# High weights by both activation halves as one product of 512 columns, in the feed-forward of a two-block transformer kernel

## The chip, the cores and the metric

One Trainium2 chip, one core. The metric is the device time of one execution in microseconds (us). The kernel before takes 2200.33 us (median of 3 runs, 2199.25 to 2201.02).

## What is computed

Two blocks over 256 tokens of width 1024 (and 256 context tokens in the first): a first block with attention, convolution and a mixture of 32 experts in each of two layers, then a second block of two hybrid layers. The edit is in the feed-forward of a hybrid layer:

```python
D_FF = 4 * D_MODEL            # 4096
def hybrid_layer(x, ..., w_ff1, w_ff2):
    ...
    hf = rms_norm(x, norm_g[2])
    ff = jnp.square(jax.nn.relu(hf @ w_ff1)) @ w_ff2
    return x + rms_norm(ff, norm_g[3])
```

All of it is in float32, and the kernel keeps that accuracy with products of rounded parts: a value x is split into high = rounded x and low = x - high, and a product w.x is the sum of w_high.x_high, w_high.x_low and w_low.x_high.

## The kernel before

The hybrid layers' weights are streamed in slabs of 128 x 4096 float32 (2 MB), one DMA each, into three ring places; a slab in use goes through `split_both` (L2987) on VectorE: a cast into `w_hi` (L2995; two places, used in turn) and a subtraction into `w_lo`, over the raw slab (L2996). The split of slab n+2 waits until TensorE is done with slab n.

The order of the feed-forward's slabs is written out in `FF_ORDER` (L87): first-half slabs (w = 1, eight a layer, 512 hidden units each) and second-half slabs (w = 2) alternate, as (1,0), (1,1), (2,0), (1,2), (2,1), ... (1,7), (2,6), (2,7). Slab (1,0) is done in `first_hidden` with tokens as output rows, and stays as it is.

For j = 1 to 7, `hidden(n, j)` (L2326) computes four chunks of 128 hidden units by 256 tokens, into the lower half (256 columns) of PSUM banks 4 to 7. A chunk is eight steps k, and a step is `three` (L1427): three products of 256 columns, L1429 (high weights by high activations), L1430 (high by low), L1431 (low by high). The activations are `hn_hi` (in the ring's last place) and `hn_lo` (in `hT`). TensorE signals each chunk by `f1_mm`.

VectorE's loop (L3182) takes the chunks of a first-half slab in order: L3192 takes the chunk m out of PSUM, max with 0 and times the row factor `rB`, into `sqb`, and signals `f1_ev`; ScalarE (L1386 to L1389) waits for that, squares in place and signals `ffh_ready`; VectorE then, after L3192 of chunk m+1, makes the parts of chunk m with `parts` (L3035): a cast into `ff_hi` (L3037), `link` (a wait for the instruction's own end), a subtraction into `ff_lo` (L3038). After a slab's four chunks VectorE goes on to the next `split_both`.

`output(n, j, b, h)` (L2346) multiplies `ff_hi` and `ff_lo` (as stationary operands) with a second-half slab, 48 products of 512 columns a slab, L2079 to L2081, into banks 0 to 3. At the end of a layer the order is: three quarters of slab (2,6), half of (2,7), the last quarter of (2,6), the rest of (2,7). `take` (L2083) makes TensorE wait until a slab is split.

In the same trace `h_lo` of the first mixer is `[P, TG, KC, NX]`, read as two runs of 256 columns with other data between, while `h_hi` is read as one run of 512.

Of the kernel before, what the change touches and what calls it, by code (L numbers as in the profile page):

```python
# [12 lines left out]
F32 = mybir.dt.float32  # L13
# [4 lines left out]
ALU = mybir.AluOpType  # L18
ACT = mybir.ActivationFunctionType
AX_X = mybir.AxisListType.X  # L20

P = 128
D = 1024
KC = D // P
NX = 256
# [60 lines left out]
SLAB = 4096  # L86
# [16 lines left out]
def hybrid_program(nc, xT_in, params_in, consts_in, invcnt_in, lparams_in, pos_in, w_static, ex_gate, ex_up, ex_down, w_layer, gains_in,  # L103
# [3 lines left out]
    lo, n_lp = offsets(LPARAMS)  # L107
    ctx = ExitStack()
    with ctx:
        address = {}  # L110
# [5 lines left out]
        def rounded(name, shape, over, column):  # L116

            return nc.alloc_sbuf_tensor_at(name, shape, FR, offset=address[over] + 4 * column)

        def sem(name):  # L120
            return ctx.enter_context(nc.semaphore(name))


        ring = sb("ring", [P, RING, SLAB])
        xT = sb("xT", [P, TG, KC, NX])
        hT = sb("hT", [P, TG, KC, NX])
        cat = sb("cat", [P, 8, 512])
        sqb = sb("sqb", [P, 4, 512])
# [13 lines left out]
        condv = sb("condv", [P, KC, 54])  # L142
# [5 lines left out]
        ps = ctx.enter_context(nc.psum_tensor("ps", [P, 8, 512], F32))  # L148

        def pc(name, a=0, n=None):  # L150
            at, w = po[name]
            return par[:, at + a:at + (w if n is None else a + n)]
# [106 lines left out]

        w_hi = rounded("w_hi", [P, 2, SLAB], "E", 0)  # L260
        w_lo = [rounded(f"w_lo{r}", [P, SLAB], "ring", r * SLAB) for r in range(RING)]
        hn_hi = rounded("hn_hi", [P, KC, NX], "ring", 5 * SLAB)
        hn_lo = rounded("hn_lo", [P, KC, NX], "hT", 0)
        ff_hi = rounded("ff_hi", [P, 8, NX], "xT", KC * NX)
        ff_lo = rounded("ff_lo", [P, 8, NX], "cat", 4 * 512)
        onsa_hi = rounded("onsa_hi", [P, 4, NX], "cat", 0)
# [29 lines left out]
        rB = stdv[:, 0:NX]  # L296
# [4 lines left out]
        cos2, sin2 = trig[:, 0, :], trig[:, 1, :]  # L301
# [14 lines left out]

        slab_in = [sem(f"slab_in{r}") for r in range(RING)]
        setup_done = sem("setup_done")
        cond_ready = sem("cond_ready")
        mod_mm = sem("mod_mm")  # L320
        mod_ev = sem("mod_ev")
        mod_fold = sem("mod_fold")
# [72 lines left out]
        mix_ready = sem("mix_ready")  # L395
        yt_mm = sem("yt_mm")
        x2_ready = sem("x2_ready")
        trig_done = sem("trig_done")
        trig_ready = sem("trig_ready")

        cmp_in = sem("cmp_in")
# [22 lines left out]
        mhi_ready = sem("mhi_ready")  # L424
        f1_mm = sem("f1_mm")
        f1_ev = sem("f1_ev")
        ffh_ready = sem("ffh_ready")
        ffs_ready = sem("ffs_ready")
        f2_mm = sem("f2_mm")
# [36 lines left out]
        for n, x in enumerate(AB_LOADS):  # L466
            r = n if n < RING else AB_SLOT[AB_FREED[n - RING]]
# [50 lines left out]
        F2, F2_ROWS = 11, (7, 10)  # L518
# [298 lines left out]
        def g2(row):  # L817
            return row.rearrange("p (g t) -> p g t", g=TG)
# [38 lines left out]
        def _(act):  # L857
# [93 lines left out]
            act.wait_ge(inputs_in, 16 * n_in)  # L951

            act.wait_ge(setup_done, 1)
            act.activation(condv[:, :, 22:24], pc("cond").rearrange("p (k c) -> p k c", c=2), ACT.Silu).then_inc(cond_ready, 1)

            def trig():
                act.wait_ge(trig_ready, 1)
                act.activation(sin2, sin2, ACT.Sin)
                act.activation(cos2, cos2, ACT.Sin).then_inc(trig_done, 1)

            def high_part(j):
                raw, hi, _ = ab_parts(j)
# [304 lines left out]
            def layer2(i):  # L1267
# [61 lines left out]
                for s in range(HEADS + 2):  # L1329
# [10 lines left out]
                    if s >= 2 and s % 2 == 1:  # L1340
                        c = (s - 2) // 2
# [4 lines left out]
                for j in range(KC // 2):  # L1346
                    m = mg.rearrange("p (b m) t -> p b m t", b=2)[:, :, 2 * j:2 * j + 2, :]
# [35 lines left out]
                for b in range(QT):  # L1383
                    act.wait_ge(ht_mm, TURNED0 + 2 * i + b + 1)
                    act.activation(ff_hi[:, 0:4, b * P:b * P + P], ps[:, 1 + b, :].rearrange("p (c t) -> p c t", c=4), ACT.Copy).then_inc(rt_ev, 1)
                for m in range(4, FF // P):  # L1386
                    act.wait_ge(f1_ev, 32 * i + m + 1)
                    r = sqb[:, m % 4, 0:NX]
                    act.activation(r, r, ACT.Square).then_inc(ffh_ready, 1)  # L1389

                post(i, 1, 0)
# [21 lines left out]
        def _(pe):  # L1413
# [13 lines left out]
            def three(out, hi, lo, xhi, xlo, first, last):  # L1427

                pe.matmul(out, hi, xhi, start=first, stop=False)  # L1429
                pe.matmul(out, hi, xlo, start=False, stop=False)  # L1430
                return pe.matmul(out, lo, xhi, start=False, stop=last)  # L1431
# [54 lines left out]
            def block1(layer):  # L1486
# [13 lines left out]
                if full:  # L1500
                    wq = 512
                    norm()
                    pe.wait_ge(cond_ready, 1)
                    for j in range(MOD0):
                        mod_sum(0, j)
                        if j < MOD0 - 1:
# [183 lines left out]
                for s in range(len(units) + 2):  # L1690
# [12 lines left out]
                    if full and 1 <= s <= 4:  # L1703
# [3 lines left out]
                        for q in (2 * s - 2, 2 * s - 1):  # L1707
                            for a in range(4):
                                ins = pe.matmul(g2(ps[32 * a:32 * a + 32, 6, :]), stacked_w[:, 4 * q + a, :], stacked[:, a, :, 4 * q:4 * q + NX],
                                                start=q == 0, stop=q == 7)  # L1710
# [390 lines left out]
            def layer2(i):  # L2101
# [58 lines left out]
                for v in range(2):  # L2160
                    pe.wait_ge(cmp_in, 48 + 16 * (2 * i + 2))
                    for j in range(CB // 2):
                        q = j % 4
# [78 lines left out]
                for s in range(HEADS + 2):  # L2242
# [15 lines left out]
                    if s >= 2:  # L2258
                        c, t = (s - 2) // 2, s % 2
# [66 lines left out]
                def hidden(n, j):  # L2326
                    hi, lo = take(i, J_FF + n)

                    def part(c, k):
                        return three(ps[:, 4 + c, 0:NX], hi[:, k, c * P:c * P + P], lo[:, k, c * P:c * P + P], hn_hi[:, k, :], hn_lo[:, k, :],  # L2330
                                     k == 0, k == KC - 1)

                    for c in range(4):
                        pe.wait_ge(f1_ev, 32 * i + 4 * j + c - 3)
                        for k in range(KC):
                            ins = part(c, k)
                        ins.then_inc(f1_mm, 1)
                        if j == 1 and c == 0:
                            pe.wait_ge(r_diag, 2 * i + 2)
                            for b in range(QT):  # L2340
                                ins = pe.matmul(ps[:, 0, b * P:b * P + P], ones[:, :], dg[:, b, :], start=True, stop=True)
                            ins.then_inc(qss_mm, 1)
                            for b in range(QT):
                                turn_hidden(b)
# [32 lines left out]
                        output(n, 7, 1, 0).then_inc(f2_mm, 1)  # L2377
                        output(n, 7, 1, 1, (lambda: turn_x(1, 0, 0)) if i == 0 else None).then_inc(f2_mm, 1)

            pe.wait_ge(trig_done, 1)  # L2380
            pe.wait_ge(inputs_in, 48 + 16)
            for i in range(2):
                layer2(i)
# [3 lines left out]
        def _(dve):  # L2387
            chain = [0]

            def link(ins):  # L2390
                chain[0] += 1
                ins.then_inc(dchain, 1)
                dve.wait_ge(dchain, chain[0])
# [641 lines left out]
            def parts(hi, lo, x):  # L3035

                link(dve.tensor_copy(hi, x))  # L3037
                return dve.tensor_tensor(lo, x, hi.bitcast(F32), ALU.subtract)  # L3038

            def layer2(i):  # L3040
# [141 lines left out]
                for n, (w, j) in enumerate(FF_ORDER):  # L3182
                    if w == 1 and j >= 1:
                        if j == 1:
                            dve.wait_ge(rb_ready, i + 1)
                        if j >= 2:
                            dve.wait_ge(f2_mm, F2 * i + j - 1)
                        for c in range(5):
                            m = 4 * j + c
                            if c < 4:  # L3190
                                dve.wait_ge(f1_mm, 32 * i + m + 1)
                                dve.scalar_tensor_tensor(sqb[:, m % 4, 0:NX], ps[:, 4 + m % 4, 0:NX], 0.0, rB, ALU.max, ALU.mult).then_inc(f1_ev, 1)  # L3192
                            if c >= 1:
                                m -= 1
                                dve.wait_ge(ffh_ready, 32 + 32 * i + m + 1)
                                parts(ff_hi[:, m % 8, :], ff_lo[:, m % 8, :], sqb[:, m % 4, 0:NX]).then_inc(ffs_ready, 1)
                    if n + 2 < len(FF_ORDER):
                        split_both(i, J_FF + n + 2)
                if i == 1:
# [217 lines left out]
```

## Time and profile before

| | |
|---|---|
| median of 3 runs | 2200.33 us (2199.25 to 2201.02) |
| profiled execution | 2204.34 us, span 2202.6 us |
| TensorE busy | 1889.1 us (86%) |
| VectorE busy | 1054.8 us (48%) |
| ScalarE busy | 558.1 us (25%) |
| mean granted TensorE clock | 0.954 |

The span holds the first block up to about 1430 us and the two hybrid layers behind it; their feed-forwards lie at about 1644 to 1812 us and 2026 to 2195 us. PE is TensorE, PEld its weight loads, DVE VectorE, ACT ScalarE. A matmul's time in the trace is from its start to its modelled end, so that consecutive ones overlap; what one costs in a stream is the distance between starts. In a timeline, a value in brackets is the engine's idle time before the row and what ended it. The granted clock (PEclk) is 1.00 at 2.4 GHz and 0.50 at 1.2 GHz; a value between is a stretch that holds both.

### The profile page before, as it was taken

Reading aid. Unit: us, or ns where it says so; the run is one execution under the profiler, and the core shown is the slowest. Engines: PE = TensorE matmul, PEld = TensorE weight load, DVE = VectorE, ACT = ScalarE, POOL = GpSimd, SP = SyncE. Lnnn points to the kernel's source line nnn. Section 1 sums busy time; section 2 is a strip of 40 time slices with the busy share of each in tenths; the row PEclk is TensorE's granted clock in tenths of the full one; section 3 lists DMA queues with packets and bytes.
Section 4 is the critical chain, followed back from the end, with each engine's and each line's share of the span. In section 5 each row is a group of like instructions: output and inputs, shape, how many; then the busy total and the mean of one; then the engine's idle time right before and its main releaser. Section 6 shows DMA issues by size and latency. Waiting matters only on the chain.

```text
span 2202.6 us, 38471 instructions
## 1 busy us (share of the span) xinstructions
PE 1889.1 (86%) x15600; PEld 1371.7 (62%) x15600; DVE 1054.8 (48%) x1955; ACT 558.1 (25%) x1189; POOL 13.6 (1%) x21
## 2 busy tenths in 40 slices
PE   7999987787867779897776766699999999999998
PEld 4744654444433447664444433398989989998997
DVE  5678541010100136642111111277878787788876
ACT  4436631111111123531111101214440012444001
POOL 0000000000000010000000000000000000000000
PEclk9999999999989999998888888899999999999999
DMA  8289359999899994359999999952354446234552
GB/s 357 77 329 428 122 188 415 422 422 430 324 430 428 415 362 167 154 205 421 428 428 428 428 428 428 384 221 86 123 203 180 186 167 262 78 138 188 191 191 96
DMA packets 51558, 625.60 MB, mean 284 GB/s; under 512 B 6912, under 2 KB 7936, under 8 KB 13440
## 3 DMA queue, kind: packets, MB, share of 16 engines
q1 hardware_dynamic: 44864, 611.30, 67.8%
q0 software_dynamic: 1792, 6.29, 0.9%
q10 hardware_dynamic: 4800, 6.56, 0.8%
q8 instruction: 75, 1.23, 0.2%
q14 instruction: 27, 0.22, 0.0%
HBM read 614.43 MB, written 9.70 MB: 283 GB/s over the span
## 4 chain that ended last, share of the span: by engine, by line
PE 54%; DMA 31%; DVE 10%; issue 2%; ACT 2%; SPq 1%; POOL 0%; ACTq 0%; POOLq 0%; DVEq 0%
DMA ring<-in_ex_gate 14%; DMA ring<-in_ex_up 13%; PE ps L1913 9%; PE ps L1429 7%; PE ps L1431 6%; PE ps L1430 6%; PE ps L2079 4%; PE ps L2081 4%; PE ps L2080 4%; DMA ring<-in_ex_down 2%; PE ps L1786 1%; DMA ring<-in_w_layer 1%; PE ps L1452 1%; DVE w_lo L2996 1%; PE ps L1814 1%
## 5 line engine op out<-in xcount | busy, mean ns | idle before, releaser
L1913 PE MATMUL ps<-ring,E 128*32 128x256 f32 x5312 | 362.7, 434 | 187.3 <-DMA ring<-in_ex_gate 119.2
L1913 PEld LDWEIGHTS ps<-ring,E 128*32 128x32 f32 x5312 | 211.3, 125 | 346.1 <-issue 277.5
L1431 PE MATMUL ps<-hn_hi,w_lo 128*128 128x256 f32 x928 | 262.3, 283 | 0.0
L2885 DVE TENSOR_TENSOR E<-E,ps 128x256 f32<-128x256 f32 x25 | 10.5, 421 | 372.7 <-PE ps L1913 372.7
L1920 PE MATMUL ps<-ring,E 128*32 128x512 f32 x1344 | 159.7, 616 | 31.3 <-DMA ring<-in_ex_down 29.9
L1431 PEld LDWEIGHTS ps<-hn_hi,w_lo 128*128 128x128 f32 x928 | 177.7, 192 | 0.0
L1429 PE MATMUL ps<-hn_hi,w_lo 128*128 128x256 f32 x480 | 138.2, 288 | 1.7 <-DVE w_lo L2996 1.7
L1430 PE MATMUL ps<-hn_lo,w_lo 128*128 128x256 f32 x480 | 135.6, 283 | 0.0
L2996 DVE TENSOR_TENSOR w_lo<-ring,w_hi 128x4096 fp32r<-128x4096 f32 x30 | 132.8, 4426 | 1.0
L1429 PE MATMUL ps<-hn_hi,w_hi 128*128 128x256 f32 x448 | 126.9, 283 | 0.0
L1430 PE MATMUL ps<-hn_lo,w_hi 128*128 128x256 f32 x448 | 126.8, 283 | 0.0
L1139 ACT ACTIVATE hT<-ps 128x512 f32<-128x512 f32 x58 | 34.6, 597 | 329.8 <-PE ps L1878 329.8
L1920 PEld LDWEIGHTS ps<-ring,E 128*32 128x32 f32 x1344 | 44.5, 113 | 116.1 <-issue 111.1
L2079 PE MATMUL ps<-w_hi,ff_hi 128*128 128x512 f32 x256 | 100.0, 391 | 0.8 <-DVE w_lo L2996 0.8
L2080 PE MATMUL ps<-w_hi,ff_lo 128*128 128x512 f32 x256 | 99.8, 390 | 0.0
L2081 PE MATMUL ps<-w_lo,ff_hi 128*128 128x512 f32 x256 | 99.6, 389 | 0.0
L1429 PEld LDWEIGHTS ps<-hn_hi,w_lo 128*128 128x128 f32 x480 | 91.7, 191 | 3.4 <-DVE w_lo L2996 2.5
L1430 PEld LDWEIGHTS ps<-hn_lo,w_lo 128*128 128x128 f32 x480 | 91.8, 191 | 0.1
L1389 ACT ACTIVATE sqb<-sqb 128x256 f32<-128x256 f32 x56 | 22.2, 418 | 264.6 <-DVE sqb L3192 264.6
L1429 PEld LDWEIGHTS ps<-hn_hi,w_hi 128*128 128x128 f32 x448 | 85.9, 192 | 0.6
L1430 PEld LDWEIGHTS ps<-hn_lo,w_hi 128*128 128x128 f32 x448 | 85.9, 192 | 0.5
L2891 DVE COPY wsl<-ps 128x1 f32<-128x1 f32 x16 | 2.5, 158 | 171.0 <-PE ps L1959 171.0
(572 smaller groups left out, 3511.3 us busy)
## 6 DMA issues: line engine op xcount, KB each, us to landing
ring<-in_ex_up SPq DMA_DIRECT2D x64, 2048.0 KB, 18.7
ring<-in_ex_gate SPq DMA_DIRECT2D x62, 2048.0 KB, 17.8
ring<-in_ex_down SPq DMA_DIRECT2D x61, 2048.0 KB, 19.2
ring<-in_w_layer SPq DMA_DIRECT2D x56, 2048.0 KB, 8.3
ring<-in_w_static SPq DMA_DIRECT2D x33, 2048.0 KB, 15.5
y_rows<-E ACTq DMA_DIRECT2D x100, 64.0 KB, 7.6
ring<-in_ex_down SPq DMA_DIRECT2D x6, 1024.0 KB, 19.1
E<-in_w_layer SPq DMA_DIRECT2D x2, 2048.0 KB, 12.4
```

Of the source, the lines that this page charges most:

```text
L1139: act.activation(xtok[:, c * 512:c * 512 + 512], ps[:, tok_row_bank(l, c, first), :], ACT.Copy).then_inc(sems["xtok_ready"], 1)
L1389: act.activation(r, r, ACT.Square).then_inc(ffh_ready, 1)
L1429: pe.matmul(out, hi, xhi, start=first, stop=False)
L1430: pe.matmul(out, hi, xlo, start=False, stop=False)
L1431: return pe.matmul(out, lo, xhi, start=False, stop=last)
L1452: ins = pe.matmul(ps[32 * u:32 * u + 32, 6 if q == 0 else 7, :], condv[:, k, at:at + 32], w[:, k, :], start=j == j0 and k < 4, stop=j == j ...
L1913: ins = pe.matmul(ps[lane(u, h), 2 + w, 0:HALF], xg[:, k, lane(u, h) if j is None else quad(j, u)], weights[u][:, h * HALF:(h + 1) * HALF] ...
L1920: ins = pe.matmul(ps[lane(u, c), bank, :], hid[:, m % 2, lane(u, m // 2)], slab(4 + u, (EC, D))[:, m, half_cols(c)], start=m == 0, stop=m ...
L2079: pe.matmul(out, xhi, hi, start=first, stop=False)
L2080: pe.matmul(out, xlo, hi, start=False, stop=False)
L2081: return pe.matmul(out, xhi, lo, start=False, stop=last)
L2996: dve.tensor_tensor(lo_flat(i, j), raw_of(i, j), hi_flat(i, j).bitcast(F32), ALU.subtract).then_inc(split_dve, 1)
```

## The change

Both activation parts become one view `hn_both` of two halves (the addresses stay). A step of `hidden` is two products instead of three: high weights by both parts, 512 columns, into both halves of the bank, and low weights by high activations, 256 columns, into the lower half. ScalarE copies the upper half of each chunk into `sqb` and signals `fb_ready`; VectorE waits for it, adds it to the lower half, waits for that, and does max and times `rB` from SBUF. ScalarE squares twice: once into `ff_hi` (in place of VectorE's cast), once in place. Two semaphores of other places are made one to free a number. `g2` views a row of 512 columns as two of 256.

```diff
-        hn_hi = rounded("hn_hi", [P, KC, NX], "ring", 5 * SLAB)
-        hn_lo = rounded("hn_lo", [P, KC, NX], "hT", 0)
+        hn_both = rounded("hn_both", [P, 2, (address["hT"] - address["ring"]) // 4 - 5 * SLAB], "ring", 5 * SLAB)
+        hn_hi, hn_lo = (hn_both[:, q, 0:KC * NX].rearrange("p (k t) -> p k t", k=KC) for q in range(2))
...
-        cond_ready = sem("cond_ready")
+        act_tables = sem("act_tables")
...
-        trig_done = sem("trig_done")
...
+        fb_ready = sem("fb_ready")
...
                 for m in range(4, FF // P):
+                    act.wait_ge(f1_mm, 32 * i + m + 1)
+                    act.activation(sqb[:, m % 4, NX:512], ps[:, 4 + m % 4, NX:512], ACT.Copy).then_inc(fb_ready, 1)
                     act.wait_ge(f1_ev, 32 * i + m + 1)
+                    if m >= 8 and m % 4 == 0:
+                        act.wait_ge(f2_mm, F2 * i + m // 4 - 1)
                     r = sqb[:, m % 4, 0:NX]
+                    act.activation(ff_hi[:, m % 8, :], r, ACT.Square)
                     act.activation(r, r, ACT.Square).then_inc(ffh_ready, 1)
...
                     def part(c, k):
-                        return three(ps[:, 4 + c, 0:NX], hi[:, k, c * P:c * P + P], lo[:, k, c * P:c * P + P], hn_hi[:, k, :], hn_lo[:, k, :],
-                                     k == 0, k == KC - 1)
+                        pe.matmul(g2(ps[:, 4 + c, :]), hi[:, k, c * P:c * P + P], hn_both[:, :, k * NX:k * NX + NX], start=k == 0, stop=False)
+                        return pe.matmul(ps[:, 4 + c, 0:NX], lo[:, k, c * P:c * P + P], hn_hi[:, k, :], start=False, stop=k == KC - 1)
...
-            pe.wait_ge(trig_done, 1)
+            pe.wait_ge(act_tables, 2)
...
                             if c < 4:
+                                r = sqb[:, m % 4, 0:NX]
                                 dve.wait_ge(f1_mm, 32 * i + m + 1)
-                                dve.scalar_tensor_tensor(sqb[:, m % 4, 0:NX], ps[:, 4 + m % 4, 0:NX], 0.0, rB, ALU.max, ALU.mult).then_inc(f1_ev, 1)
+                                dve.wait_ge(fb_ready, 28 * i + m - 3)
+                                link(dve.tensor_tensor(r, ps[:, 4 + m % 4, 0:NX], sqb[:, m % 4, NX:512], ALU.add))
+                                dve.scalar_tensor_tensor(r, r, 0.0, rB, ALU.max, ALU.mult).then_inc(f1_ev, 1)
                             if c >= 1:
                                 m -= 1
                                 dve.wait_ge(ffh_ready, 32 + 32 * i + m + 1)
-                                parts(ff_hi[:, m % 8, :], ff_lo[:, m % 8, :], sqb[:, m % 4, 0:NX]).then_inc(ffs_ready, 1)
+                                dve.tensor_tensor(ff_lo[:, m % 8, :], sqb[:, m % 4, 0:NX], ff_hi[:, m % 8, :].bitcast(F32), ALU.subtract).then_inc(ffs_ready, 1)
```

## Rows read from the trace of the kernel before

**Rows 1.** The page: busy times, and the chain that ended last.

```profile
PE 1889.1 (86%) x15600; PEld 1371.7 (62%) x15600; DVE 1054.8 (48%) x1955; ACT 558.1 (25%) x1189; POOL 13.6 (1%) x21
...
PE 54%; DMA 31%; DVE 10%; issue 2%; ACT 2%; SPq 1%; POOL 0%; ACTq 0%; POOLq 0%; DVEq 0%
```

**Rows 2.** Stretches: a period of feed-forward; last columns granted clock, DMA share, GB/s.

```profile
core 0: us, PE busy (x) PEld busy (x) DVE busy (x) ACT busy (x) POOL busy (x), PEclk, DMA share, GB/s
1700.00:1722.42 22.42, 22.42 (x146) 20.53 (x146) 17.46 (x17) 1.58 (x4) 0.00 (x0) 1.00 0.50 188
```

**Rows 3.** Waits, 1650 to 1803 us: total us, times, longest us.

```profile
DVE w_hi L2995 <- PE ps L2081: 13.4, 6, 2.6
...
PE ps L2079 <- DVE w_lo L2996: 0.4, 1, 0.4
```

**Rows 4.** TensorE's timeline, starts of slabs (2,j) and (1,j+2): start us, us.

```profile
1701.63 0.40 PE L2079 MATMUL ps<-w_hi,ff_hi 128*128 128x512 f32 x1
...
1712.54 0.28 PE L1429 MATMUL ps<-hn_hi,w_hi 128*128 128x256 f32 x1
```

**Rows 5.** TensorE's timeline in the first mixer.

```profile
59.98 0.39 PE L1430 MATMUL ps<-h_lo,w_lo 128*128 128x512 f32 x1
60.21 0.39 PE L1431 MATMUL ps<-h_hi,w_lo 128*128 128x512 f32 x1
```

**Rows 6.** VectorE's timeline in one period: split, chunks, next split.

```profile
1712.81 2.30 DVE L2995 CAST w_hi<-ring 128x4096 fp32r<-128x4096 f32 x1 [2.56 <-PE ps L2081]
...
1719.48 0.74 DVE L3192 SCALAR_TENSOR_TENSOR sqb<-ps,stdv 128x256 f32<-128x256 f32 x2
1720.38 0.29 DVE L3037 CAST ff_hi<-sqb 128x256 fp32r<-128x256 f32 x1 [0.15 <-ACT sqb L1389]
1720.71 0.42 DVE L3038 TENSOR_TENSOR ff_lo<-sqb,ff_hi 128x256 fp32r<-128x256 f32 x1
1721.37 0.42 DVE L3192 SCALAR_TENSOR_TENSOR sqb<-ps,stdv 128x256 f32<-128x256 f32 x1 [0.24 <-PE ps L1431]
```

**Rows 7.** ScalarE: its timeline, and a group by form (count, busy us, mean ns).

```profile
1719.93 0.75 ACT L1389 ACTIVATE sqb<-sqb 128x256 f32<-128x256 f32 x2 [17.22 <-DVE sqb L3192]
...
L1389 ACT ACTIVATE sqb<-sqb 128x256 f32<-128x256 f32 x56 | 22.2, 418 | 264.6 <-DVE sqb L3192 264.6
...
L1271 ACT ACTIVATE E<-ps 128x256 f32<-128x256 f32 x36 | 13.6, 382 | 47.9 <-PE ps L1431 47.9
```

**Rows 8.** The page's groups: a sum or product with a PSUM operand.

```profile
L2885 DVE TENSOR_TENSOR E<-E,ps 128x256 f32<-128x256 f32 x25 | 10.5, 421 | 372.7 <-PE ps L1913 372.7
```

**Rows 9.** VectorE's timeline at a layer's first regular slab.

```profile
1656.45 0.75 DVE L3192 SCALAR_TENSOR_TENSOR sqb<-ps,stdv 128x256 f32<-128x256 f32 x2
...
1660.67 2.29 DVE L2995 CAST w_hi<-ring 128x4096 fp32r<-128x4096 f32 x1
1662.99 4.43 DVE L2996 TENSOR_TENSOR w_lo<-ring,w_hi 128x4096 fp32r<-128x4096 f32 x1
```

**Rows 10.** TensorE's timeline: starts of slabs (1,2) and (2,7).

```profile
1667.69 0.28 PE L1429 MATMUL ps<-hn_hi,w_hi 128*128 128x256 f32 x1
...
1800.07 0.47 PE L2079 MATMUL ps<-w_hi,ff_hi 128*128 128x512 f32 x1 [0.41 <-DVE w_lo L2996]
```

**Rows 11.** TensorE's timeline: waits of 2 to 4 us elsewhere.

```profile
218.54 1.79 PE L1676 MATMUL ps<-E 128*64 128x128 f32 x16 [2.28 <-ACT E L947]
...
306.62 0.27 PE L1855 MATMUL ps<-con,E 128*1 128x64 f32 x2 [3.29 <-DVE E L2772]
...
1414.82 1.92 PE L1920 MATMUL ps<-ring,E 128*32 128x512 f32 x16 [2.71 <-DMA ring<-in_ex_down]
```

**Rows 12.** Stretches behind those waits: columns as in rows 2.

```profile
218.00:224.00 6.00, 5.46 (x40) 3.37 (x40) 0.00 (x0) 1.68 (x3) 0.00 (x0) 0.72 1.01 429
...
305.00:310.00 5.00, 3.38 (x11) 2.60 (x12) 4.68 (x17) 0.00 (x0) 0.00 (x0) 0.75 0.01 3
...
1415.00:1417.00 2.00, 2.00 (x18) 0.56 (x10) 0.00 (x0) 0.00 (x0) 0.00 (x0) 1.00 0.98 416
```

## What I expect of the change, and why

> **What bounds the kernel now.** I read the busy line and the chain of waits first: TensorE is busy for 86% of the span and holds 54% of the chain, and DMA's 31% belongs to the expert blocks, which the edit leaves alone [rows 1]. The edit lives in the feed-forward of the two hybrid layers. There the stretches show TensorE busy all the time, at the upper clock level, over a pattern that repeats every 22.42 us: one slab of first-half weights and one of second-half weights. VectorE is busy 17.46 of the 22.42 us [rows 2]. The waits of one layer's stretch say who has room: VectorE waits for TensorE before a weight split (6 times, up to 2.6 us), TensorE waits for VectorE once, 0.4 us [rows 3]. So TensorE bounds this stage, and VectorE has 4.96 us a period in hand, on average. Whether that room lies where the edit needs it is the question.
>
> **TensorE's saving.** The timeline gives slab starts. The 48 products of 512 columns of a second-half slab run from 1701.63 to 1712.54, 0.2273 us each. The period less those 10.91 us leaves 11.51 us for 96 products of 256 columns, 0.1199 us each [rows 2, 4]. A step (one k of one chunk) is three of these now, and will be one of 512 and one of 256: 2 x 0.1199 - 0.2273 = 0.0125 us less. A slab has 32 steps: 0.40 us less (11.11 us). Fourteen slabs (seven a layer, the first of a layer is done another way and stays) would give 5.6 us.
>
> The new product reads its 512 columns as two runs far apart. The first mixer has such products: h_lo is read as two runs, h_hi as one, and 0.23 us pass from one to the next all the same [rows 5]; I take the two runs at nothing. The low-weight product of 256 columns is costed as now. The address of either half does not move, and the renamed semaphore is waited for at the same events; both nothing.
>
> The Trainium skill (TensorE: Matmul & The Clock Gate, Back-to-back issue gap) puts the warm gap at the streaming time plus about 2.5 ns, so that a merged product would save 2.5 ns and 448 of them 1.1 us. The rows here show 12.5 ns, and the sum goes by them.
>
> **What VectorE and ScalarE get.** Now VectorE's work on a chunk is one multiply-max, a cast, and a subtraction; ScalarE squares in between. Durations: 0.42 multiply-max, 0.29 cast (0.33 to the next, linked, instruction), 0.42 subtraction [rows 6]; square 0.42, the second of two starting 0.33 after the first (0.75 for both) [rows 7]. The edit takes the cast off VectorE, and puts on it a sum of a PSUM half and an SBUF copy with a link. The trace has no such line here; a 128x256 TENSOR_TENSOR with a PSUM operand elsewhere takes 0.421 us [rows 8], so 0.42 + 0.04 for the link = 0.46 against the cast's 0.33: +0.13 us a chunk, 0.5 us a slab. That alone would vanish in the 4.96 us. ScalarE gets a copy out of PSUM, 0.382 us for that size [rows 7], and a second square.
>
> But the order on the two queues makes a ring. ScalarE copies the upper half of chunk m, then waits for VectorE's result on m, squares twice, and only then copies for m+1; VectorE's sum for m+1 waits for that copy. Behind this wait stand the subtraction of m and, at the end, the next weight split, which TensorE waits for. Once TensorE has done several chunks, one turn of the ring is: sum 0.46, multiply-max 0.42 + 0.03 to ScalarE (1719.48 to 1719.93 [rows 6, 7]), two squares 0.33 + 0.33, copy 0.38 + 0.03 = 1.98 us. A block of four chunks is three turns (5.94), then 0.46 + 0.45, 0.33 + 0.42 + 0.03 for the last two squares (the second one releases), and 0.34 for the subtraction: 7.97 us. Now it is 4.22 us where nothing else delays it (1656.45 to 1660.67 [rows 9]). Three places decide:
>
> (a) *The first regular slab of a layer.* All four chunks are there when VectorE comes, at 1656.45, and its split after them (cast and, 2.32 later, 4.43 us of subtraction: 6.75) ends at 1667.42, just before TensorE starts the next first-half slab at 1667.69 [rows 9, 10]. With the edit: the first chunk is 0.1 earlier, so 1656.35 + 7.97 + 6.75 = 1671.07. TensorE starts at 1671.1 instead of 1667.69: +3.4 us. It would have been ready at 1667.4: a wait of 3.7 us that is not there now.
>
> (b) *The steady periods.* From the start of a first-half slab (1712.54) VectorE begins a split 0.27 later and the chunks 6.94 later [rows 4, 6]. 6.94 + 7.97 + 6.75 = 21.66 us, and TensorE wants that split at 11.11 + 10.91 = 22.02. It fits by 0.36 us. Chunk 3 is copied in time (TensorE has it at 11.3, the ring asks for it at 12.5). So these five periods keep their gain: 5 x 0.40 = -2.0 us. An extra 0.1 us on a turn would use up the room, and each further 0.1 costs 0.4 us a period.
>
> (c) *The last slabs.* After the last first-half slab TensorE has only 36 products before it needs the last split. Now: 11.51 + 8.18 = 19.69 us after that slab's start, and it waits 0.41 us [rows 10]: 20.10. With the edit the split comes at 21.69, TensorE is ready at 11.11 + 8.18 = 19.29: a wait of 2.4 us, +1.6 us against now.
>
> A layer: +3.4 - 2.0 + 1.6 = +3.0 us; both: +6.0 us. What follows the last split (output rows, statistics, the next layer's pieces) hangs on TensorE and moves as a whole.
>
> **TensorE's clock.** The rows have waits of this size between busy stretches. After one of 2.28 us (to 218.54) and one of 3.29 us (to 306.62) the granted clock of the stretch is 0.72 and 0.75, a mix of both levels (2.4 and 1.2 GHz); after one of 2.71 us (to 1414.82) it stays at 1.00 [rows 11, 12]. A fall costs (1 - 0.72) x 6 = 1.7 us, at 305 to 310 (1 - 0.75) x 5 = 1.25. The waits of 3.7 us in (a) are longer than all three, so I take a fall at each: 2 x 1.7 = +3.4 us. TensorE is the bound again right behind them, so it counts in full. For (c), with 2.4 us, it is open: 0 to +3.4 more for both layers, and not in the forecast. The same page of the Trainium skill (HAM oscillation) warns of idle gaps in a stream of matmuls; "the default state is throttled, and activity releases the throttle". By it these gaps are not only lost time; rows 11 and 12 agree in two of three.
>
> **The sum.** +6.0 + 3.4 = +9.4 us. On the profiled execution (2204.34 us with its span of 2202.6) that is 2213.7; that execution lies 4.0 us above the median of the runs, so for the median it is 2200.33 + 9.4 = 2209.7 us.
>
> **Rivals.**
>
> 1. *The ring as computed, and the clock holds.* +6.0: 2206.3 us. For it: one of three waits. Against: the two others, shorter than 3.7.
>
> 2. *The ring is slower than its parts and decides each period too.* Waits and hand-offs that now never stand in a row could cost 0.05 to 0.3 us more a turn. With +0.2: a block is 0.8 us longer; (a) +0.8, (c) +0.8, and the five periods 0.8 - 0.36 = 0.44 each, 2.2: +3.8 a layer, 2209.7 + 7.6 = 2217.3 us. It decides from +0.1 a turn. Against: the hand-offs above are read from the same pair of engines.
>
> 3. *TensorE stays the bound: faster.* If the ring hid behind TensorE everywhere, all 5.6 us come: 2194.7 us. For it: 4.96 us free a period. Against: in (a) VectorE is now only 0.3 us early, and in (c) already 0.4 us late; any lengthening shows. It decides from a block of at most 1667.38 - 6.75 - 1656.35 = 4.3 us, with two engines alternating four times in it.
>
> 4. *Partly hidden, no change that can be told.* With a turn of 1.6 us in place of 1.98 (a sum and a copy cheaper than their nearest rows) a block is 4 x 0.38 = 1.5 us shorter: (a) falls to +1.9, in (c) the split comes at 20.1, as now, +0.0, and a layer is -0.1: 2200.1 us, if the clock holds. Against: all four pieces of the turn have rows of the same size.
>
> 5. *The merged product is not faster.* If 512 columns in two runs into one bank took 0.24 us, 5 x 0.40 would be lost a layer and (a), (c) stay, since VectorE sets them: 2209.7 + 4.0 = 2213.7 us. Against: rows 5. (The page's 2.5 ns would lie close to this: 0.32 of each 0.40 lost, 2212.9 us.)
>
> **Chances.** Forecast 0.42, with the clock at (c) open (2209.7 to 2213); rival 1 0.2; rival 2 0.15; rival 3 0.08; rival 4 0.1; rival 5 0.05. About 0.2% (4.4 us) is what a measurement of this kernel can tell from no change. Slower by more holds the forecast, 1, 2 and 5, less a little of 1 that could come out under +4.4: 0.8. Within: 0.12. Faster: 0.08. The range goes from 2203 (the clock holds, and a turn is 0.2 us shorter: 0.8 less in (a) and in (c), 3.2 for both layers, 2206.3 - 3.2) to 2218 (rival 2 at +0.2); it leaves out rivals 3 and 4, 0.18 together.
>
> **What would show it.** TensorE's timeline in a layer's feed-forward: a wait of about 3.7 us before the second first-half slab of a layer, released by the weight split, and of 2.4 us before the last second-half slab; none in between. Period 22.0 us. VectorE's block of four chunks about 8 us, sums 2.0 us apart, each released by ScalarE's copy. A granted clock below 1.00 behind the long waits. The prediction is wrong if the sums come closer than 1.5 us, if TensorE waits in every period, or if the steps of one 512 and one 256 product take more than 0.35 us.

## The result, and the profile after

The changed kernel is slower: 2214.91 us (median of 10 runs, 2209.04 to 2220.53) against 2200.78 us (10 runs, 2197.64 to 2208.31); the ratio over all runs is 1.0055, 95% interval 1.0044 to 1.0067, which is 10 to 15 us (the two medians lie 14.1 us apart). The forecast was 2209.7 us with a range of 2203 to 2218.

The profiled execution of the changed kernel took 2209.04 us with a span of 2207.3 us, only 4.7 us over the span before. That is a trap: the two executions differ by 7 us in the first block, whose work the edit leaves as it was. The first full weight split of the first hybrid layer's feed-forward starts at 1642.61 us here and at 1649.79 before. From that point to the end of the span it is 2207.3 - 1642.61 = 564.7 us against 2202.6 - 1649.79 = 552.8 us: +11.9 us, in line with the timed ratio. So I measure a *stretch* below: from the start of VectorE's cast of slab (2,0) (before: 1649.79) to TensorE's start of slab (2,7) (before: 1800.07 [rows 10]). Before it is 150.28 us in the first layer and 150.23 in the second; after, 1798.83 - 1642.61 = 156.22 and 156.00. A wait in brackets counts from the modelled end of the product before it, and in a stream the next product would have started 0.17 us before that end (a product of 512 columns lasts 0.40 us and the next one starts after 0.23). So a wait costs the stream about 0.2 us more than its bracket says.

Waits of TensorE in both hybrid layers, after (total us, times, longest us); before it waited 0.4 us once a layer for a split here [rows 3, 10]:

```profile
PE ps L2335 <- DVE w_lo L3001: 7.0, 2, 3.5
PE ps L2084 <- DVE w_lo L3001: 4.4, 2, 2.2
```

Each layer waits 3.5 us for a weight split before its second regular first-half slab (L2335 is the merged product), and 2.2 us before slab (2,7). VectorE's timeline up to the first of these waits answers to rows 9:

```profile
1649.27 0.42 DVE L3199 TENSOR_TENSOR sqb<-ps,sqb 128x256 f32<-128x256 f32 x1
1649.72 0.42 DVE L3200 SCALAR_TENSOR_TENSOR sqb<-sqb,stdv 128x256 f32<-128x256 f32 x1
1651.28 0.43 DVE L3199 TENSOR_TENSOR sqb<-ps,sqb 128x256 f32<-128x256 f32 x1 [1.13 <-ACT sqb L1388]
...
1653.30 0.42 DVE L3199 TENSOR_TENSOR sqb<-ps,sqb 128x256 f32<-128x256 f32 x1 [0.80 <-ACT sqb L1388]
...
1655.31 0.43 DVE L3199 TENSOR_TENSOR sqb<-ps,sqb 128x256 f32<-128x256 f32 x1 [0.80 <-ACT sqb L1388]
...
1656.99 0.42 DVE L3204 TENSOR_TENSOR ff_lo<-sqb,ff_hi 128x256 fp32r<-128x256 f32 x1 [0.46 <-ACT sqb L1394]
1657.33 2.28 DVE L3000 CAST w_hi<-ring 128x4096 fp32r<-128x4096 f32 x1
1659.65 4.42 DVE L3001 TENSOR_TENSOR w_lo<-ring,w_hi 128x4096 fp32r<-128x4096 f32 x1
```

The sums (L3199) come 2.01 us apart, each but the first after an idle time that ScalarE's copy (L1388) ends. The block takes 1657.33 - 1649.27 = 8.06 us; before, 4.22. ScalarE's timeline shows one turn:

```profile
1650.18 0.42 ACT L1393 ACTIVATE ff_hi<-sqb 128x256 fp32r<-128x256 f32 x1 [8.11 <-DVE sqb L3200]
1650.50 0.40 ACT L1394 ACTIVATE sqb<-sqb 128x256 f32<-128x256 f32 x1
1650.81 0.36 ACT L1388 ACTIVATE sqb<-ps 128x256 f32<-128x256 f32 x1
1652.20 0.42 ACT L1393 ACTIVATE ff_hi<-sqb 128x256 fp32r<-128x256 f32 x1 [1.02 <-DVE sqb L3200]
```

The copy for the next chunk stands behind both squares, though its data have been in PSUM for microseconds. TensorE's timeline after the wait, and the stretch behind it (columns as in rows 2):

```profile
1664.13 0.50 PE L2335 MATMUL ps<-hn_both,w_hi 128*128 128x512 f32 x1 [3.49 <-DVE w_lo L3001]
...
1665.82 0.63 PE L2335 MATMUL ps<-hn_both,w_hi 128*128 128x512 f32 x1
1666.25 0.41 PE L2336 MATMUL ps<-hn_both,w_lo 128*128 128x256 f32 x1
1666.46 0.63 PE L2335 MATMUL ps<-hn_both,w_hi 128*128 128x512 f32 x1
```

```profile
1665.00:1672.00 7.00, 7.00 (x33) 6.06 (x32) 6.46 (x4) 0.82 (x3) 0.00 (x0) 0.78 0.30 128
```

A step takes 0.64 us here, and in a steady period it takes the following, with the clock at 1.00:

```profile
1710.59 0.40 PE L2335 MATMUL ps<-hn_both,w_hi 128*128 128x512 f32 x1
1710.82 0.28 PE L2336 MATMUL ps<-hn_both,w_lo 128*128 128x256 f32 x1
1710.94 0.40 PE L2335 MATMUL ps<-hn_both,w_hi 128*128 128x512 f32 x1
1711.18 0.28 PE L2336 MATMUL ps<-hn_both,w_lo 128*128 128x256 f32 x1
1711.30 0.40 PE L2335 MATMUL ps<-hn_both,w_hi 128*128 128x512 f32 x1
```

From 1710.59 to 1711.30 two steps take 0.71 us. Over the whole slab, from its first start at 1710.25 to that of the next slab at 1721.54, it is 11.29 us or 0.353 a step, where the forecast had 0.347 and the kernel before has 0.360. The period is the distance between splits that TensorE releases:

```profile
1732.75 2.29 DVE L3000 CAST w_hi<-ring 128x4096 fp32r<-128x4096 f32 x1 [0.76 <-PE ps L2086]
...
1754.98 2.29 DVE L3000 CAST w_hi<-ring 128x4096 fp32r<-128x4096 f32 x1 [0.76 <-PE ps L2086]
```

22.23 us, against 22.42 before: 0.19 us saved, not 0.40.

### The profile page after: what moved, and what is told of

It reads as the page before. It is cut to its first block, busy times and chain, and to the rows that moved or that the text cites. A ratio compares the mean times of both kernels' runs of the same rounds, so it can differ in the third digit from the quotient of the medians.

```text
span 2207.3 us, 37741 instructions
## 1 busy us (share of the span) xinstructions
PE 1890.1 (86%) x15152; PEld 1347.7 (61%) x15152; DVE 1063.9 (48%) x1955; ACT 593.8 (27%) x1301; POOL 13.5 (1%) x21
## 4 chain that ended last, share of the span: by engine, by line
PE 50%; DMA 31%; DVE 12%; issue 3%; ACT 2%; SPq 1%; POOL 0%; ACTq 0%; DVEq 0%; POOLq 0%
DMA ring<-in_ex_gate 13%; DMA ring<-in_ex_up 13%; PE ps L1918 9%; PE ps L1434 4%; PE ps L1436 4%; PE ps L1435 4%; PE ps L2335 4%; PE ps L2084 3%; PE ps L2086 3%; PE ps L2085 3%; DMA ring<-in_ex_down 2%; PE ps L2336 2%; DVE w_lo L3001 2%; DMA ring<-in_w_layer 2%; PE ps L1791 1%
## 5 line engine op out<-in xcount | busy, mean ns | idle before, releaser
L2335 PE MATMUL ps<-hn_both,w_hi 128*128 128x512 f32 x448 | 161.6, 403 | 7.0 <-DVE w_lo L3001 7.0
L1434 PE MATMUL ps<-hn_both,w_lo 128*128 128x256 f32 x480 | 138.2, 288 | 1.6 <-DVE w_lo L3001 1.6
L1435 PE MATMUL ps<-hn_both,w_lo 128*128 128x256 f32 x480 | 135.6, 283 | 0.0
L1436 PE MATMUL ps<-hn_both,w_lo 128*128 128x256 f32 x480 | 135.5, 282 | 0.0
L2336 PE MATMUL ps<-hn_both,w_lo 128*128 128x256 f32 x448 | 127.1, 284 | 0.0
L2335 PEld LDWEIGHTS ps<-hn_both,w_hi 128*128 128x128 f32 x448 | 85.7, 191 | 28.6 <-DVE w_lo L3001 7.8
L1434 PEld LDWEIGHTS ps<-hn_both,w_lo 128*128 128x128 f32 x480 | 91.7, 191 | 3.4 <-DVE w_lo L3001 2.4
L1435 PEld LDWEIGHTS ps<-hn_both,w_lo 128*128 128x128 f32 x480 | 91.8, 191 | 0.1
L1436 PEld LDWEIGHTS ps<-hn_both,w_lo 128*128 128x128 f32 x480 | 91.8, 191 | 0.0
L2336 PEld LDWEIGHTS ps<-hn_both,w_lo 128*128 128x128 f32 x448 | 86.1, 192 | 0.5
L3000 DVE CAST w_hi<-ring 128x4096 fp32r<-128x4096 f32 x30 | 68.6, 2288 | 9.5 <-PE ps L2086 9.5
```

The costliest lines, as they stand in the source:

```text
L2335: pe.matmul(g2(ps[:, 4 + c, :]), hi[:, k, c * P:c * P + P], hn_both[:, :, k * NX:k * NX + NX], start=k == 0, stop=False)
L2336: return pe.matmul(ps[:, 4 + c, 0:NX], lo[:, k, c * P:c * P + P], hn_hi[:, k, :], start=False, stop=k == KC - 1)
L3000: link(dve.tensor_copy(hi_flat(i, j), raw_of(i, j)))
```

## The experiments

All are read by the stretch (first, second layer) and the period. "Changed" is the changed kernel. In the code cuts `...` stands for what is left out.

| kernel | period | stretch | ratio to before (95%) |
|---|---|---|---|
| before | 22.42 | 150.28, 150.23 | |
| changed | 22.23 | 156.22, 156.00 | 1.0055 (1.0044 to 1.0067) |
| e1 merge alone | 22.24 | 149.13, 149.08 | 0.9994 (0.9980 to 1.0008) |
| e2 new chunk work alone | 22.39 | 158.18, 156.99 | single run |
| e3 merge, grouped | 22.05 | 148.08, 148.07 | single run |
| e4 merge, one run | 22.23 | 148.88, 148.88 | single run |
| e5 copy ahead | 22.23 | 150.74, 150.74 | 0.9997 (0.9985 to 1.0009) |
| e6 12 spare products | 22.23 | 155.89, 155.90 | 1.0051 (1.0033 to 1.0068) |
| e9 8 spare products | 22.23 | 154.66, 154.70 | single run |
| e10 changed, grouped | 22.05 | 155.34, 155.37 | single run |
| e7 copy ahead, subtraction behind | 22.23 | 149.28, 149.09 | single run |
| e8 the same, grouped | 22.05 | 148.29, 148.29 | 0.9974 (0.9964 to 0.9985) |

**The merge alone (e1).** TensorE as changed; `parts` and the single square as before. The upper half of a bank is not read, so the kernel leaves out high weights by low activations in seven slabs a layer; only its time is of use. The same holds for e3 and e4.

```diff
-    act.activation(sqb[:, m % 4, NX:512], ps[:, 4 + m % 4, NX:512], ACT.Copy).then_inc(fb_ready, 1)
...
-    act.activation(ff_hi[:, m % 8, :], r, ACT.Square)
...
-    link(dve.tensor_tensor(r, ps[:, 4 + m % 4, 0:NX], sqb[:, m % 4, NX:512], ALU.add))
-    dve.scalar_tensor_tensor(r, r, 0.0, rB, ALU.max, ALU.mult).then_inc(f1_ev, 1)
+    dve.scalar_tensor_tensor(sqb[:, m % 4, 0:NX], ps[:, 4 + m % 4, 0:NX], 0.0, rB, ALU.max, ALU.mult).then_inc(f1_ev, 1)
...
-    dve.tensor_tensor(ff_lo[:, m % 8, :], sqb[:, m % 4, 0:NX], ff_hi[:, m % 8, :].bitcast(F32), ALU.subtract).then_inc(ffs_ready, 1)
+    parts(ff_hi[:, m % 8, :], ff_lo[:, m % 8, :], sqb[:, m % 4, 0:NX]).then_inc(ffs_ready, 1)
```

> TensorE's merged product alone; VectorE's and ScalarE's chunk work is that of the kernel before. The upper half of the bank is not read, so high weights by low activations are left out of seven slabs a layer. Theory (the ring of copies costs the time, the merge saves 0.35 us a slab less than forecast): the period is 22.2 us, as in the changed kernel's steady periods (22.23), not 22.0; no wait of 3.5 us at a layer's second first-half slab, and about 0.6 us instead of 0.41 before the last slab. From the start of a layer's first full weight split to TensorE's start of the last slab: 150.28 - 6 x 0.19 = 149.1 us (kernel before 150.28, changed kernel 156.22). Time about 2 to 3 us under the kernel before. Rival (the merged product itself slows TensorE, and the waits follow from that): the stretch stays above 153 us.

The long wait is gone and the stretch is 149.13 us: the merge is worth 1.15 us a layer. I had expected the wait before slab (2,7) to grow to 0.6 us; it is 0.38. VectorE's last chunk waits for TensorE there (1.73 us in each slab), so VectorE gets faster with it. The times show no difference: the ratio's interval is 0.28% wide, and 2.3 us are 0.1%.

**The new chunk work alone (e2).** After a chunk's first step, the high weights are multiplied by the two halves one after the other:

```diff
-    pe.matmul(g2(ps[:, 4 + c, :]), hi[:, k, ...], hn_both[:, :, k * NX:k * NX + NX], ...)
+    pe.matmul(ps[:, 4 + c, 0:NX], hi[:, k, ...], hn_hi[:, k, :], ...)
+    pe.matmul(ps[:, 4 + c, NX:512], hi[:, k, ...], hn_lo[:, k, :], ...)
```

> The changed kernel with TensorE's work unmerged: from the second step of a chunk on, three products of 256 columns again, high by low into the upper half; the copies, sums and squares are the changed kernel's. Nothing is left out. Theory (the ring): the wait of about 3.5 us at a layer's second first-half slab and about 2.0 us before the last one stay, VectorE's block of four chunks stays 8.06 us, the period is 22.4 us. The stretch of a layer is 156.2 + 0.19 x 5 = 157.2 us, with a clock fall as in the changed kernel. Rival (the merge is the cause): the waits go, 150 us.

The waits of 3.5 and 2.1 us are there without the merge, VectorE's block is 8.06 us again (1655.85 to 1663.91), the period 22.39 us. The new chunk work causes the waits. The two layers differ by 1.2 us, and the clock behind the waits accounts for it: its mean was 0.80 over 1670.7 to 1686.0 us, which is a loss of 3.1 us, and 0.89 over 2061.5 to 2077.0, a loss of 1.7.

**Where half of the merge's saving stays (e3, e4).** e3 puts a chunk's products of equal width together, e4 reads the moving data as one run:

```diff
     for k in range(KC):
-        ins = part(c, k)
+        pe.matmul(g2(ps[:, 4 + c, :]), hi[:, k, ...], hn_both[:, :, k * NX:k * NX + NX], start=k == 0, stop=False)
+    for k in range(KC):
+        ins = pe.matmul(ps[:, 4 + c, 0:NX], lo[:, k, ...], hn_hi[:, k, :], start=False, stop=k == KC - 1)
```

```diff
-    pe.matmul(g2(ps[:, 4 + c, :]), hi[:, k, ...], hn_both[:, :, k * NX:k * NX + NX], ...)
+    pe.matmul(g2(ps[:, 4 + c, :]), hi[:, k, ...], g2(hn_both[:, 0, x:x + 512]), ...)      # x = min(k, 6) * NX
```

> As the merge alone (upper half not read), but in each chunk the eight products of 512 columns come first and then the eight of 256. If the missing half of the saving is lost at each change from a 256-column product to one of 512 (0.234 us for that one, 0.2273 inside a run of them), the slab falls from 11.32 to 11.1 us and the period from 22.2 to 22.0 us. If it is lost to the two runs of the moving data, or to the 512-column product as such, the period stays 22.2 us.

> As the merge alone, but the moving data of the 512-column product is one contiguous run (two neighbouring k of the high activations), so the products are of other data and only the time counts. If the two runs cost the missing half of the saving, the period falls from 22.2 to 22.0 us; if the change between widths costs it, it stays 22.2 us.

VectorE's splits that TensorE releases, merge alone, then grouped, then one run:

```profile
1683.11 2.29 DVE L2995 CAST w_hi<-ring 128x4096 fp32r<-128x4096 f32 x1 [2.60 <-PE ps L2081]
...
1705.35 2.29 DVE L2995 CAST w_hi<-ring 128x4096 fp32r<-128x4096 f32 x1 [2.60 <-PE ps L2081]
```

```profile
1686.36 2.29 DVE L2997 CAST w_hi<-ring 128x4096 fp32r<-128x4096 f32 x1 [2.56 <-PE ps L2081]
...
1708.41 2.29 DVE L2997 CAST w_hi<-ring 128x4096 fp32r<-128x4096 f32 x1 [2.56 <-PE ps L2081]
```

```profile
1686.00 2.29 DVE L2995 CAST w_hi<-ring 128x4096 fp32r<-128x4096 f32 x1 [2.58 <-PE ps L2081]
...
1708.23 2.29 DVE L2995 CAST w_hi<-ring 128x4096 fp32r<-128x4096 f32 x1 [2.60 <-PE ps L2081]
```

22.24, 22.05 and 22.23 us. In these periods the two runs of the moving data cost nothing, and grouping gives back 0.19 us: the first-half slab falls from 11.29 to 11.15 us, and the second-half slab behind it from 10.94 to 10.91.

Alternating widths are not the whole cause, though. In e4 the first of the six slabs, (1,2), has the same alternating products and takes 11.10 us, and only the later ones take 11.29. Starts of (1,2), of (2,1) behind it, of (1,3) and of (2,2):

```profile
1663.71 0.39 PE L2330 MATMUL ps<-hn_both,w_hi 128*128 128x512 f32 x1
...
1674.81 0.39 PE L2079 MATMUL ps<-w_hi,ff_hi 128*128 128x512 f32 x1
...
1685.73 0.39 PE L2330 MATMUL ps<-hn_both,w_hi 128*128 128x512 f32 x1
...
1697.02 0.40 PE L2079 MATMUL ps<-w_hi,ff_hi 128*128 128x512 f32 x1
```

That slab has 0.347 us a step, the forecast's price, and it is the same in the second layer; in e1 it takes 11.29 and 11.30 us. This is also why e4's stretch is 0.2 us shorter than e1's. So grouping removes the loss wherever it was tried (e3, e8, e10), while the alternating products of e4 ran once a layer without it. What decides between the two is open. A hint of the loss was in the trace of before, in TensorE's timeline at the start of a second-half slab behind products of 256 columns (the line left out, at 1701.63, is that of [rows 4]):

```profile
1701.51 0.28 PE L1431 MATMUL ps<-hn_hi,w_lo 128*128 128x256 f32 x1
...
1701.87 0.40 PE L2080 MATMUL ps<-w_hi,ff_lo 128*128 128x512 f32 x1
1702.10 0.39 PE L2081 MATMUL ps<-w_lo,ff_hi 128*128 128x512 f32 x1
```

0.24 and 0.23 us there, 0.2273 on average over the slab. At a resolution of 0.01 us this is no more than a hint.

**The ring (e5).** ScalarE's order inside a slab, nothing else:

```diff
     for m in range(4, FF // P):
-        act.wait_ge(f1_mm, 32 * i + m + 1)
-        act.activation(sqb[:, m % 4, NX:512], ps[:, 4 + m % 4, NX:512], ACT.Copy).then_inc(fb_ready, 1)
+        if m % 4 < 3:
+            upper(m + 1)       # the same wait and copy, for chunk m + 1
         act.wait_ge(f1_ev, 32 * i + m + 1)
```

> The changed kernel with one thing moved: inside a slab ScalarE copies the upper half of chunk m+1 before it waits for VectorE's result on chunk m, so that the sum of m+1 no longer waits for the squares of m. Same work on every engine. Theory (the ring, not the amount of work, makes the block long): VectorE's block of four chunks at a layer's second first-half slab falls from 8.06 to about 5.2 us, TensorE's wait there from 3.5 to 0.9 us, the wait before the last slab from 2.2 to 1.1 us, no clock fall behind them, period 22.2 us. A layer's stretch (start of the first full split to TensorE's start of the last slab) 150.4 us against 156.2 with the change and 150.3 before; time within 1 us of the kernel before. Rival (the added work itself, 0.13 us of VectorE and 0.7 us of ScalarE a chunk): the block stays over 7 us and the waits stay.

Same instructions, another order, and 5.3 to 5.5 us a layer are back. VectorE's block is 5.15 us, the sums no longer wait, only the last subtraction does:

```profile
1654.54 0.42 DVE L3206 TENSOR_TENSOR sqb<-ps,sqb 128x256 f32<-128x256 f32 x1
...
1655.34 0.41 DVE L3206 TENSOR_TENSOR sqb<-ps,sqb 128x256 f32<-128x256 f32 x1
...
1659.35 0.42 DVE L3211 TENSOR_TENSOR ff_lo<-sqb,ff_hi 128x256 fp32r<-128x256 f32 x1 [0.46 <-ACT sqb L1399]
1659.69 2.29 DVE L3007 CAST w_hi<-ring 128x4096 fp32r<-128x4096 f32 x1
```

TensorE's waits are 0.6 and 1.2 us, the granted clock over 1655 to 1680 us is 1.00, and the time is that of the kernel before (0.9997). The ring's order, not the added work, makes the changed kernel slower than before; of the 5.3 to 5.5 us, 1.3 to 1.6 are the clock's fall, as e9 shows below. The added work still has a price: e5's stretch is 1.6 us longer than that of the merge alone. I had 150.4 us for the stretch and it is 150.74.

**The clock (e6, e9).** Spare products in the wait of 3.5 us, which change no result:

```diff
     def hidden(n, j):
+        if j == 2:
+            pe.wait_ge(f1_ev, 32 * i + 4 * j - 3)
+            spin(12, 4)          # e9: spin(8, 4)
         hi, lo = take(i, J_FF + n)
```

> The changed kernel with 12 spare products of TensorE (about 0.24 us each, into a bank whose content is taken already and is started anew behind them) in the wait of 3.5 us at a layer's second first-half slab. They change no result. Theory (the idle time lowers the clock, and that costs 1.6 us a layer): the wait is filled, granted clock 1.00 in the 8 us behind it, and a layer's stretch is 156.2 - 1.6 = 154.6 us; 3.2 us less than the changed kernel in all. Rival (the clock's fall costs nothing here, VectorE being late anyway): clock 1.00 but the stretch stays 156 us.

e6 was mis-sized. 12 spare products took 5.0 us, more than the wait:

```profile
1665.12 5.34 PE L1430 MATMUL ps<-ones 128*128 128x256 f32 x24
1670.12 0.58 PE L2338 MATMUL ps<-hn_both,w_hi 128*128 128x512 f32 x1
```

The split was done at about 1668.7, so the slab started 1.4 us late, and that ate the gain: clock 1.00, stretch 155.9. e6 alone would have fitted the rival that the clock costs nothing.

> As the run with spare products in the wait, with 8 in place of 12. There one took 0.417 us (5.0 us for 12), so they overran the wait and started the slab 1.4 us late; 8 of them take 3.3 us of the 3.6 us wait. Theory (the clock's fall costs 1.6 us a layer): TensorE starts the slab when the split is done, granted clock 1.00 behind it, and the layer's stretch is 156.2 - 1.6 = 154.6 us. Rival (the fall costs nothing): 156 us with the clock at 1.00.

With 8 the slab starts at 1671.94, which is 21.52 us after the first split, exactly as in the changed kernel; the clock stays up, and the stretch is 154.66 and 154.70 us. Against 156.22 and 156.00 the fall cost 1.56 and 1.30 us. Behind the slab's start, where the changed kernel had 0.78:

```profile
1672.00:1680.00 8.00, 8.00 (x45) 6.97 (x46) 7.28 (x4) 1.00 (x3) 0.00 (x0) 1.00 0.38 163
```

But e9 does not end earlier than the changed kernel. The stretch ends at slab (2,7), and behind that slab's wait, 2.2 us in both, the clock fell in both layers of e9 and in neither of the changed kernel. The 7 us behind it in the first layer, changed kernel, then e9:

```profile
1798.80:1805.80 7.00, 6.97 (x31) 5.78 (x32) 4.72 (x6) 1.97 (x6) 0.00 (x0) 1.00 0.00 0
```

```profile
1805.10:1812.10 7.00, 7.00 (x24) 5.64 (x25) 4.18 (x5) 0.98 (x3) 0.00 (x0) 0.76 0.00 0
```

From TensorE's start of the last slab (2,7) to the end of the span it is 2207.3 - 2187.55 = 19.75 us in the changed kernel and 2216.4 - 2195.04 = 21.36 in e9, so this fall costs 1.6 us too. From the first split to the end of the span e9 takes 566.0 us against 564.7. In e6 the clock fell behind the same wait in the first layer and not in the second, which ends in 19.79 us.

**Does VectorE's ring fit into a steady period (e10)?** The changed kernel with e3's grouping, so that TensorE asks for the splits 0.18 us earlier:

> The changed kernel with only the products of a chunk grouped (eight of 512 columns, then eight of 256); copies, sums and squares as in the changed kernel. Theory (VectorE's ring leaves 0.3 us in a steady period, as forecast): the period is 22.05 us, as in the grouped merge without the new chunk work; the waits at the first and last place are 3.6 and 2.4 us; the stretch is 156.1 - 5 x 0.18 = 155.2 us with a clock fall. Rival (the ring already decides the periods): the period stays 22.2 us with a short wait of TensorE in each.

```profile
1714.31 2.29 DVE L3002 CAST w_hi<-ring 128x4096 fp32r<-128x4096 f32 x1 [0.57 <-PE ps L2086]
...
1736.36 2.29 DVE L3002 CAST w_hi<-ring 128x4096 fp32r<-128x4096 f32 x1 [0.58 <-PE ps L2086]
```

The period is 22.05 us, VectorE still idle for 0.57 us in it, and TensorE waits only at the two known places (3.5 and 2.4 us). The ring fits. The clock fell behind all four waits, also behind those of 2.4 us (0.76 over 7 us).

**Can both be had (e7, e8)?** e7 is e5 with the subtraction of a slab's last chunk moved behind the next split; e8 has e3's grouping besides. Both compute all of it.

```diff
-                            if c >= 1:
+                            if 1 <= c < 4:
...
                         split_both(i, J_FF + n + 2)
+                    if w == 1 and j >= 1:
+                        m = 4 * j + 3
+                        dve.wait_ge(ffh_ready, 32 + 32 * i + m + 1)
+                        dve.tensor_tensor(ff_lo[:, m % 8, :], sqb[:, m % 4, 0:NX], ff_hi[:, m % 8, :].bitcast(F32), ALU.subtract).then_inc(ffs_ready, 1)
```

> The copy ahead, and in addition the subtraction of a slab's last chunk moved behind the next weight split on VectorE. Theory: the block at a layer's second first-half slab is 4.3 us, TensorE's wait there under 0.15 us; at the last slab the split comes at about 19.7 us after the last first-half slab's start and the last subtraction 0.4 later, so TensorE starts at 20.1, about as in the kernel before. Stretch 149.1 us. Rival (some of the waits are the work's own): a wait over 0.5 us stays at the first place.

> The copy ahead, the last subtraction behind the split, and the products of a chunk in groups (eight of 512 columns, then eight of 256). Theory: period 22.05 us as in the grouped merge alone, no wait over 0.2 us at the first place, stretch 148.1 us a layer; 4.3 us less than the kernel before over both layers, 0.998 of its time. Rival (VectorE or ScalarE keep part of it): the stretch stays at 149 us or more, and the time is that of the kernel before within 0.1%.

e7 has 149.28 and 149.09 us; its wait at the first place is gone, and 0.6 us are left before slab (2,7), where it now waits for the moved subtraction. e8 has 148.29 in both layers, 1.9 to 2.0 us less than before in each, and is faster than the kernel before: 2197.49 us (median of 8 runs) against 2203.55 us (19 runs of the kernel before beside them), ratio 0.9974 (0.9964 to 0.9985). The traces account for 3.9 of the 5.7 us of the ratio, which is inside the interval (3 to 8 us); the rest I can't place. TensorE's waits for VectorE in e8's first layer:

```profile
PE ps L2091 <- DVE hn_both L3042: 1.1, 1, 1.1
PE ps L2091 <- DVE ff_lo L3219: 0.6, 1, 0.6
PE ps L2110 <- DVE hT L3037: 0.4, 1, 0.4
```

The block that decides is 4.27 us (1652.55 to 1656.82), under the 4.3 us that the forecast named as the point where TensorE stays the bound. The 0.6 us at slab (2,7) are left here too.

## Why the prediction was right, and where its sizes were off

**Which engine bounds, and where its cover ends.** Right. VectorE's 4.96 us of room a period were of no use at the two places where it is short.

**The ring.** Right: 2.01 us a turn against 1.98, a block of 8.06 against 7.97. e5 shows that it is the cause. Every piece came from a row of the same engine and size. One hand-off was too cheap: VectorE's sum starts 0.11 us after ScalarE's copy has ended (1650.81 + 0.36 to 1651.28), not 0.03; the squares and the copy itself were a little shorter than their rows.

**(a) the first regular slab.** The forecast had a wait of 3.7 us; the bracket has 3.5, and counted from where the next product would have started it is 3.65. From the start of the first split to TensorE's start of the slab it is 1664.13 - 1642.61 = 21.52 us, against 1667.69 - 1649.79 = 17.90: +3.6 us, where the forecast had +3.4. The first chunk did not start 0.1 us earlier, as the forecast had it: VectorE comes to it 6.66 us after the start of the first split in both kernels (1649.27 - 1642.61; 1656.45 - 1649.79), when it is done with that split. The rest is the longer block and a hand-off.

**(b) the steady periods.** Right that the ring fits; the term was mis-sized. The saving is 0.19 us a period, not 0.40: over five periods -0.95 us a layer in place of -2.0. The step that failed is the one that took 2 x 0.1199 - 0.2273 from products in runs of equal width and used it for alternating ones. The prediction named a step of more than 0.35 us as a sign that it is wrong, and the step takes 0.353: that sign did appear, against this term. The range still holds the result, since the term is small beside the waits. The whole merge, had nothing stood against it, is worth 2.3 us (e1), not 5.6; grouped, 4.4 us (e3).

**(c) the last slabs.** Forecast +1.6 us. The last first-half slab starts 0.27 us before the split that TensorE releases, at 1776.94 (split at 1777.21), and slab (2,7) starts 21.89 us later; before 20.28 us (1800.07 less 1667.69 + 5 x 22.42): +1.6. The prediction's own figures were 21.69 and 20.10. For the kernel before it added the bracket of 0.41 us to products counted by the distance of their starts, which leaves out the 0.17 us between the two ways of counting. The error is about the same on both sides, so the difference came out right partly by luck. The bracket has 2.2 instead of 2.4 us because the slab itself is 0.2 us longer than forecast; in e10, where it is not, it has 2.4.

**The clock.** Forecast 1.7 us at each wait of 3.7 us. e9 shows 1.56 and 1.30. It fell behind all six such waits in the changed kernel, e2 and e10. Behind the waits before slab (2,7) the forecast left it open, and it is: the clock stayed at 1.00 in both layers of the changed kernel and of e2, and fell in one of e6 and in both of e9 and e10. The profiled execution of the changed kernel is the shortest of its ten, so others may hold such falls; no trace shows them. The sentence of the Trainium skill that the prediction quotes, on the default state, stands in the same page's section What's actually happening, and not under HAM oscillation.

**The sum.** A layer +3.6 - 0.95 + 1.6 + 1.4 = +5.7 us; the two measured ones are +5.9 and +5.8. Forecast: +3.0 + 1.7 = +4.7. For both, 11.9 us to the end of the span against 9.4. Of the missing 2.5 us the steady periods are 2.1, place (a) is 0.4, and the clock took back 0.5; the rest is rounding and lies behind the stretches. The medians' 14.1 us hold 2.2 more, which no trace places. Of the rivals, 1 (the clock holds) falls by e9, 2 (the ring decides each period) by e10, 3 and 4 by the trace. Rival 5 (the merge not faster) was half true: 0.353 us a step lies midway between its 0.360 and the forecast's 0.347. The Trainium skill's gap (TensorE: Matmul & The Clock Gate, Back-to-back issue gap), streaming time plus 2.5 ns, which the page gives for an isolated gap, makes an estimate of 1.1 us for the merges. The runs show 2.3 us alternating and 4.4 us grouped, so neither is near it, and the measurement decides.

## What to carry to other kernels

When two engines that each work through a list in order hand work to each other chunk by chunk, add up one turn of the ring, not each engine's busy time: an evacuation copy that needs nothing but PSUM belongs ahead of the wait for the other engine's answer. Look for the places where the bounding engine's cover is shortest (the first period and the last), since room that exists on average does not help there. And cost a product in the sequence in which it will stand: a price read from a run of equal ones need not hold when two widths alternate. Last, when an experiment shifts the work in time, read the whole span too: e9 won 1.3 to 1.6 us a layer in the stretch and lost it behind the stretch.

## What the runs showed of the hardware that I had not expected

- Alternating products of 512 and 256 columns cost 0.19 us a period of 32 pairs more than the same products grouped by width (22.24 against 22.05 us). It is not so in every slab: with the moving data in one run, slab (1,2) took 11.10 us in both layers of e4 and the later slabs 11.29. Reading 512 columns as two runs far apart costs nothing in the steady periods (22.24 against 22.23 us with one run).
- A wait of TensorE of 3.5 us in a dense stretch was followed by a lower clock six times out of six (mean 0.78 over 7 us in the first layer of the changed kernel) and cost 1.3 to 1.6 us beyond the wait. Of six waits of 2.2 us (changed kernel, e6, e9) three were followed by a fall; where it could be read at the end of the span, it cost 1.6 us.
- A spare product of 256 float32 columns whose operands are not of the rounded type took 0.417 us and shows as two matmuls each, against 0.12 us for a product of rounded parts.
